# Cached keys turned by VectorE and attention biases added by VectorE in a streaming encoder

## What is computed

```python
q, k, v = split(x @ w_in); lf = log_sigmoid(x @ w_f + b_f)     # 16 heads of 64
c = cumsum(concat([cache_lf, lf]), axis=1)                      # prompt: no cache
s = q . k_all * 64 ** -0.5                                      # k_all = [cache_k, k]
s = s + cq[:, :, :, None] - ck[:, :, None, :]
s = where(kpos <= qpos, s, -inf)
o = softmax(s) . v_all;  y = o @ w_out
```

## Time and profile before

| | |
|---|---|
| runs, median (lowest to highest) | 1886.13 us (1880.18 to 1888.01) |
| profiled execution, first to last instruction | 1885.1 us |
| profiled execution, time around the span | none listed apart; the median of the runs is 1.0 us above the span |
| TensorE / VectorE / ScalarE / GpSimd busy | 98% / 52% / 38% / 12% |
| granted TensorE clock, mean | 0.997 |
| HBM read, written | 243.19 MB, 13.19 MB |

### The profile page before, as it was taken

One profiled execution on the slowest core, in us unless ns is written; L12 is line 12 of the kernel. 1 busy time (PEld: TensorE's weight loads), 2 busy tenths in 40 slices (PEclk: granted clock), 3 DMA queues, 4 the chain that ended last, 5 costly groups with the idle time before them and its releaser, 6 DMA issues.

```text
span 1885.1 us, 29064 instructions
## 1 busy us (share of the span) xinstructions
PE 1849.9 (98%) x12004; PEld 1642.4 (87%) x12004; DVE 983.0 (52%) x1569; ACT 722.0 (38%) x1144; POOL 225.9 (12%) x357
## 2 busy tenths in 40 slices
PE   8999999999999999999999999999999999999998
PEld 8777799998888887799998899998897777999986
DVE  4557653443567778743443664443465576543434
ACT  4246443333255454333332343333242463433321
POOL 3114070000011222230000100000031230000000
PEclk9999999999999999999999999999999999999999
DMA  7357254433353433444433434433364562444332
GB/s 246 128 203 229 81 160 123 129 129 123 117 164 105 125 116 104 118 139 125 124 134 123 146 101 125 132 124 125 110 206 150 200 221 90 137 132 124 128 129 79
DMA packets 179171, 259.38 MB, mean 138 GB/s; under 512 B 14717, under 2 KB 122349, under 8 KB 179040
## 3 DMA queue, kind: packets, MB, share of 16 engines
q1 hardware_dynamic: 161184, 197.18, 32.3%
q0 software_dynamic: 17856, 60.35, 9.9%
HBM read 243.19 MB, written 13.19 MB: 136 GB/s over the span
## 4 chain that ended last, share of the span: by engine, by line
PE 90%; DVE 4%; ACT 3%; issue 1%; DMA 1%; SPq 0%; DVEq 0%; ACTq 0%
PE ps L1605 14%; PE ps L1607 14%; PE ps L1606 14%; PE ps L1617 11%; PE ps L1615 11%; PE ps L1616 11%; PE ps L1833 1%; PE ps L1951 1%; PE ps L1938 1%; PE ps L1638 1%; PE ps L1888 1%; PE ps L1671 1%; DVE w_lo L785 1%; PE ps L1908 1%; PE ps L1673 1%
## 5 line engine op out<-in xcount | busy, mean ns | idle before, releaser
L785 DVE TENSOR_TENSOR w_lo<-w_raw,w_hi 128x1024 fp32r<-128x1024 f32 x370 | 452.1, 1228 | 709.1 <-ACT w_hi L439 707.9
L439 ACT ACTIVATE w_hi<-w_raw 128x1024 fp32r<-128x1024 f32 x370 | 389.3, 1059 | 803.5 <-DMA w_raw<-in_w_ffn_in_dram 363.1
L1605 PE MATMUL ps<-xT_hi,w_hi 128*128 128x384 f32 x1568 | 528.4, 337 | 2.5 <-issue 1.4
L1607 PE MATMUL ps<-xT_hi,w_lo 128*128 128x384 f32 x1568 | 527.0, 336 | 0.0
L1606 PE MATMUL ps<-xT_lo,w_hi 128*128 128x384 f32 x1568 | 526.9, 336 | 0.0
L1605 PEld LDWEIGHTS ps<-xT_hi,w_hi 128*128 128x128 f32 x1568 | 294.8, 188 | 5.2 <-issue 5.1
L1606 PEld LDWEIGHTS ps<-xT_lo,w_hi 128*128 128x128 f32 x1568 | 294.8, 188 | 0.1
L1607 PEld LDWEIGHTS ps<-xT_hi,w_lo 128*128 128x128 f32 x1568 | 294.8, 188 | 0.0
L1617 PE MATMUL ps<-w_hi,hT_lo 128*128 128x512 f32 x528 | 210.6, 399 | 0.0
L1616 PE MATMUL ps<-w_lo,hT_hi 128*128 128x512 f32 x528 | 208.1, 394 | 0.0
L1615 PE MATMUL ps<-w_hi,hT_hi 128*128 128x512 f32 x528 | 207.4, 393 | 0.0
(11 more groups left out here) (329 smaller groups left out, 2021.8 us busy)
## 6 DMA issues: line engine op xcount, KB each, us to landing
w_raw<-in_w_ffn_in_dram SPq DMA_DIRECT2D x352, 256.0 KB, 3.2
w_raw<-in_w_ffn_out_dram SPq DMA_DIRECT2D x176, 256.0 KB, 2.9
w_raw<-in_w_fox_in_dram SPq DMA_DIRECT2D x96, 256.0 KB, 2.9
k_c<-in_cache_fox_k_dram POOLq DMA_DIRECT2D x32, 512.0 KB, 5.3
v_c<-in_cache_fox_v_dram POOLq DMA_DIRECT2D x32, 512.0 KB, 4.0
w_raw<-in_w_hgrn_in_dram SPq DMA_DIRECT2D x64, 256.0 KB, 2.9
w_raw<-in_w_fox_out_dram SPq DMA_DIRECT2D x32, 256.0 KB, 2.9
out_dram<-kv_tok POOLq DMA_DIRECT2D x4, 1024.0 KB, 5.0
```

The costliest lines, as they stand in the source:

```text
L439: nc.scalar.activation(w_hi[:, slot, :], w_raw[:, slot, :], ACT.Copy).then_inc(hi_ready, 1)
L785: V.tensor_tensor(w_lo[:, slot, :], w_raw[:, slot, :], w_hi[:, slot, :].bitcast(F32), ALU.subtract).then_inc(lo_ready, 1)
L1605: mm(out, w_hi[:, slot, cols], x_hi[:, k, :], start=k == 0, stop=False, skip_group_check=True)
L1607: last = mm(out, w_lo[:, slot, cols], x_hi[:, k, :], start=False, stop=k == KD - 1, skip_group_check=True)
```

## The change

- The layer with `AHEAD = 3` is the second attention layer. Its cached keys are loaded by GpSimd during the feed-forward of layer 2 (8 loads of 1 MB, `cached_keys`), turned in blocks of 32x32 by VectorE (8 transposes of 128x256 in each of chunks 1 to 8, `turn_keys_ahead`), and stored turned by SP to a DRAM buffer `keys_t` (`store_turned`). In the attention loop SP loads them from there (`turned_keys`, 512 KB a set, three buffers), GpSimd adds the new keys' columns (`new_keys`), and TensorE's `s_keys` and the copies to `ktc` go.
- In both attention layers the sums are written to DRAM, read back broadcast over partitions (`load_prompt_bias`, 384 KB for two heads; `load_sample_bias`, 272 KB for a stream), masked by GpSimd, and added by VectorE in the instruction that also finds the extremum (`tensor_tensor_reduce`). Queries carry the opposite sign, so that the maximum becomes a minimum. The sum is written to SBUF, where ScalarE reads it.
- The bias and mask matmuls, and the constants and splits for them, go. TensorE's next scores wait for the extremum (`nmax`, `s_nmax`) and no longer for the exponential. In the second layer TensorE's folds move between the halves of `p_scores` and `p_out`, and the copies and low halves of the folds move later on ScalarE and VectorE.

The diff, cut to its core:

```diff
-CROWS = 64 + DT
-LAID = 17
+LAID = 4
+LOADED = 16 * 4
 KV = 3
+AHEAD = 3
+TWIN = 8
+TCOLS = 256
...
+            def turned_keys(i, first, end):
+                f = FOX[i]
+                for n in range(first, end):
+                    b, hf = n // 2, n % 2
+                    if n < KV:
+                        sync.wait_ge(*at(KEYS["stored"], 64 * DB))
+                        sync.wait_ge(unit_used, START[i]["mix"])
+                    else:
+                        sync.wait_ge(*at(f["s_scores"], n - KV + 1))
+                    sync.dma_start(k_t[:, n % KV, :, 0:PAST], keys_t[b, hf * WCOLS:(hf + 1) * WCOLS, :].rearrange(
+                        "(g p) k -> p g k", p=P)).then_inc(KEYS[f"in{n % KV}"][0], 16)
+            def store_turned(n):
+                b0, cols = 4 * (n // 4), slice(TCOLS * (n % 4), TCOLS * (n % 4) + TCOLS)
+                sync.wait_ge(*at(KEYS["turned"], n + 1))
+                for r in range(4):
+                    sync.dma_start(keys_t[b0 + r, cols, :].rearrange("(c d) k -> d c k", d=32),
+                                   k_turn[32 * r:32 * r + 32, :, :, :].rearrange("d c k a -> d c (k a)")).then_inc(KEYS["stored"][0], 16)
...
+                    if i + 1 == AHEAD and 3 <= c < CF:
+                        store_turned(c - 3)
...
+                    if i + 1 == AHEAD and 1 <= c <= DB:
+                        turn_keys_ahead(c - 1)
+            def turn_keys_ahead(n):
+                dve.wait_ge(*at(KEYS["loaded"], 16 * (n + 1)))
+                if n:
+                    dve.wait_ge(*at(KEYS["stored"], 64 * n))
+                for a in range(TWIN):
+                    ins = V.transpose(k_turn[:, :, :, a], k_nat[:, a, :])
+                ins.then_inc(KEYS["turned"][0], 1)
...
                     if 1 <= n <= HEADS:
                         dve.wait_ge(*at(f["s_scores"], n))
-                        V.tensor_reduce(nmx[:, (n - 1) % 2, 2:3], ps[:, SS_BANK, 0:PAST + DT], AX_X, ALU.max,
-                                        negate=True).then_inc(f["s_nmax"][0], 1)
+                        if n % 2:
+                            dve.wait_ge(*at(f["bias"], sample_bias(n // 2)))
+                        V.tensor_tensor_reduce(out=p_s[:, (n - 1) % 2, :], in0=ps[:, SS_BANK, 0:PAST + DT],
+                                               in1=bias_s[:, (n - 1) // 2 % 2, (n - 1) % 2, :], scale=1.0, scalar=LARGEST, op0=ALU.add,
+                                               op1=ALU.min, accum_out=nmx[:, (n - 1) % 2, 2:3]).then_inc(f["s_nmax"][0], 1)
...
                         dve.wait_ge(*at(f["scores"], n // 2 + 1))
-                        V.tensor_reduce(nmx[:, n % 2, 0:1], ps[:, bank, 0:P], AX_X, ALU.max, negate=True)
-                        V.tensor_reduce(nmx[:, n % 2, 1:2], ps[:, bank, P:T], AX_X, ALU.max,
-                                        negate=True).then_inc(f["nmax"][0], 1)
-                        if n:
+                        if n % 2 == 0:
+                            dve.wait_ge(*at(f["bias"], prompt_bias(n // 2)))
+                        for q, lo, hi in ((0, 0, P), (1, P, T)):
+                            ins = V.tensor_tensor_reduce(out=p_p[:, n % 2, lo:hi], in0=ps[:, bank, lo:hi],
+                                                         in1=bias_p[:, n // 2 % 2, n % 2, lo:hi], scale=1.0, scalar=LARGEST, op0=ALU.add,
+                                                         op1=ALU.min, accum_out=nmx[:, n % 2, q:q + 1])
+                        ins.then_inc(f["nmax"][0], 1)
+                        if n and i != AHEAD:
                             key_sides(n, KT_BANKS + 1)
...
+                def load_prompt_bias(k):
+                    pool.dma_start(bias_p[:, k % 2, :, :], sums_p[j, 2 * k:2 * k + 2, :].partition_broadcast(P)).then_inc(
+                        f["bias_in"][0], 16)
+                def load_sample_bias(b):
+                    pool.dma_start(bias_s[:, b % 2, :, :],
+                                   sums_s[j, :, b, :, :].rearrange("h f k -> h (f k)").unsqueeze(1).broadcast_to(
+                                       [HEADS // 2, DT, 2 * (PAST + DT)])).then_inc(f["bias_in"][0], 16)
+                def mask_prompt_bias(k):
+                    blocks = bias_p[:, k % 2, :, :].rearrange("p e (t c) -> p e t c", t=NTOK)[:, :, 0:NTOK:2, :]
+                    G.tensor_tensor(blocks, blocks, causal[:, :].unsqueeze(1).unsqueeze(1).broadcast_to([P, 2, 2, P]),
+                                    ALU.subtract).then_inc(f["bias"][0], 1)
+                def mask_sample_bias(b):
+                    new = bias_s[:, b % 2, :, PAST:]
+                    G.tensor_tensor(new, new, new_mask[:, :].unsqueeze(1).broadcast_to([P, 2, DT]), ALU.subtract).then_inc(
+                        f["bias"][0], 1)
+                def next_bias(m):
+                    if m:
+                        pool.wait_ge(*at(f["bias_in"], LOADED + 16 * (4 + m)))
+                        if m % 2:
+                            mask_prompt_bias(m // 2 + 2)
+                        else:
+                            mask_sample_bias(m // 2 + 1)
+                    if m < 2 * DB - 4 and m % 2 == 0:
+                        pool.wait_ge(*at(f["nmax"], m + 2))
+                        load_prompt_bias(m // 2 + 2)
+                    elif m < 2 * DB - 4:
+                        pool.wait_ge(*at(f["s_nmax"], m + 1))
+                        load_sample_bias(m // 2 + 2)
...
                 for n in range(KV, 2 * DB + KV):
-                    if n < 2 * DB:
+                    if n < 2 * DB and i == AHEAD:
+                        pool.wait_ge(*at(f["s_scores"], n - KV + 1))
+                        new_keys(n)
+                    elif n < 2 * DB:
                         pool.wait_ge(*at(f["ktr"], n - KV + 1))
                         load_k(n)
                     pool.wait_ge(*at(f["s_o"], n - KV + 1))
...
                     if n - KV + 2 < 2 * DB:
                         load_new(n - KV + 2)
+                    if n - KV <= 2 * DB - 4:
+                        next_bias(n - KV)
...
                 def p_scores(k):
-                    for e in range(2):
-                        h = 2 * k + e
-                        if k:
-                            pe.wait_ge(*at(f["exp"], h - 1))
-                        out = ps[:, S_BANK[e], 0:T]
-                        mm(out, sel_p[:, h:h + 1].broadcast_to([CROWS, P]), c_p[:, :], start=True, stop=False, skip_group_check=True)
-                        mm(out.rearrange("p (t c) -> p t c", t=NTOK)[:, 0:NTOK:2, :], ident_r[:, :],
-                           causal_r[:, :].rearrange("p (t c) -> p t c", t=NTOK)[:, 0:NTOK:2, :], start=False, stop=False,
-                           skip_group_check=True)
+                    if k:
+                        pe.wait_ge(*at(f["nmax"], 2 * k))
                     for lo, hi, n in ((0, P, P), (P, T, SEQ)):
+                        if lo and i == AHEAD and k:
+                            s_fold(2 * k - 2)
...
                 def s_pairs(n):
                     if n:
-                        pe.wait_ge(*at(f["s_exp"], n))
-                    pe.wait_ge(*at(f["kt_a"], n + 1))
-                    pe.wait_ge(*at(f["kt_d"], n + 1))
+                        pe.wait_ge(*at(f["s_nmax"], n))
+                    if i == AHEAD:
+                        pe.wait_ge(*at(KEYS[f"in{n % KV}"], 16 * (n // KV + 1)))
+                        pe.wait_ge(*at(KEYS["new"], n + 1))
+                    else:
+                        pe.wait_ge(*at(f["kt_a"], n + 1))
+                        pe.wait_ge(*at(f["kt_d"], n + 1))
...
-                    mm(ps[:, SS_BANK, 0:PAST + DT], sel_s[:, n % 2, :], c_s[:, n // 2, :], start=False, stop=True,
-                       skip_group_check=True).then_inc(f["s_scores"][0], 1)
+                    last.then_inc(f["s_scores"][0], 1)
```

More of the change, by code:

```diff
@@ L126, in trunk_program @@
         causal = sb("causal", [P, P], after("ident"))
-        ident_r = sb("ident_r", [P, P], after("causal"), F32R)
-        causal_r = sb("causal_r", [P, T], after("ident_r"), F32R)
-        fold = sb("fold", [P, 4, DT], after("causal_r"))
-        half = sb("half", [P, 2], after("fold"))
+        fold = sb("fold", [P, 4, DT], after("causal"))
+        new_mask = sb("new_mask", [P, DT], after("fold"))
+        half = sb("half", [P, 2], after("new_mask"))
         own = sb("own", [P, 2, HD], after("half"))
@@ L285, in trunk_program @@
             "z": 1, "zma": 2, "ze": 1, "zl": 1, "lf": 3, "cT": 5, "cT_ev": 5, "kT_done": KD, "kT_a": KD, "scores": KD,
[L286 removed]
+            "ones": 1, "c": 1 + DB, "laid": LAID, "bias_in": LOADED + 16 * 2 * DB, "bias": 2 * DB,
             **{k: HEADS for k in ("nmax", "exp", "rcp", "scaled", "pT", "pT_ev", "rcs")},
@@ L303, in trunk_program @@
         y_stored = sem("y_stored")
+        H = HGR[KINDS.index("hgrn")]
+        KEYS = {"loaded": (H["st0_in"][0], 16 * (HG // 2)), "stored": (x_in[0], 16),
```

(52 more changed lines are left out.)

183 lines of the change are left out of this document (96 added, 87 removed).

## The result

The change makes the kernel **slower**: 1949.04 us median (1948.4 to 1951.55, 4 runs) against 1885.43 of the kernel before on the same chip, ratio 1.0338, interval 1.032 to 1.0357. The forecast was 1871 in a range of 1860 to 1890. The profiled execution took 1948.72 us, its span 1946.7.

The account below looks back on a forecast made before the run. TensorE bounds the kernel before; after the change GpSimd's loop decides in both attention layers. Savings 6.6 + 8.9 = 15.5 us, other terms nothing: 1885.1 - 15.5 = 1869.6 traced, median 1870.6, say 1871; range 1860 to 1890.

Parts of the forecast that it names:

- The third feed-forward: VectorE's 64 key turns, 3.3 to 8.2 us a chunk, fit in 10.0 free of 16.7; SP's stores and added traffic cost nothing.
- without them each late microsecond is paid in full: Third feed-forward: without free VectorE time and the weights' lead of 21 us, each late microsecond costs its full length.
- Rival 5: Third feed-forward: turns or doubled traffic make weights late and eat the gain, 1886 us or more; chance 0.04.
- GpSimd's loop: Attention loops: one bias load in flight, landings 3.9 and 3.6 us, a pair 9.5; saves 6.6 and 8.9 us.
- it decides from about 4.5 us a landing: Attention loops: the slower outcome, Rival 4, decides once a bias load takes about 4.5 us to land.
- rivals 3: Attention loops: contention stretches both landings to 4.25 us, a pair is 10.5, 1.2 and 3.5 saved: 1881 us; chance 0.12.
- Rival 4: Attention loops: biases queue behind value loads, land in 5.3 us, a pair 12.6; 10.3 and 8.0 lost: 1904; chance 0.17.
- 3.6 us of first masks added: Before the attention loops: these masks lie beside the projection, where GpSimd idles 24.5 us, and cost nothing.
- The 34 us of matmuls: Attention loops: bias and mask matmuls, L1940 and second-layer key turns hold TensorE at most 20.0 + 14.1 = 34 us.
- by TensorE alone: Attention loops bound by TensorE: last scores end at 184.3 us (first layer) and 50.4 after the start (second), waits charged.
- A faster loop would meet it: Second attention layer: 17.8 MB of DMA at 329 GB/s take 54 us, no cost beside 59.
- Rival 2: Attention loops: sample bias moves on half the DMA engines, landing in 4.0 us for 3.6: 1875 us; chance 0.10.

Follow-up runs that it names:

- Experiment 1: Kernel after, with the stores of the turned keys issued by GpSimd behind its wait for the turns, SP neither waiting nor storing: 1911.15 us, ratio 1.0136.
- experiment 2: Experiment 1 with SP keeping its bare wait for the turns between weight loads: 1941.22 us, ratio 1.0299.
- kernel 10: The kernel of 8, with GpSimd issuing the next key load ahead of the four stores, nothing left out: 1880.08 us, ratio 0.9975.
- Experiments 3: Kernel after with the bias part alone; cached keys of the second layer turned by TensorE as in the kernel before: 1902.07 us, ratio 1.0093.
- 4: Kernel after, with GpSimd issuing the next bias load before it waits for and masks the previous, two in flight: 1930.52 us, ratio 1.0238.
- 5: Kernel after with the edits of Experiment 1 and 4 together: 1893.57 us, ratio 1.0044.
- 6: Experiment 1 without bias loads or later masks in the loops; later pairs and sets reuse the first biases, output wrong: 1875.41 us, ratio 0.9952.
- 8: Kernel before with only the keys part of the change, turned keys stored by GpSimd, biases still matmuls: 1886.65 us, ratio 1.0008.
- kernel 7: Experiment 1 with SP issuing the loop's bias loads, one of each kind in flight, GpSimd only masking: 1890.49 us, ratio 1.0035.

## Why the prediction was wrong

**The step that failed** is "The third feed-forward", which ends "I cost it at nothing". It is 39 of the 62 us. Its sizes held: the turns are 0.51 us each from start to start inside the bounds of 0.41 and 1.03, and VectorE had the time. What failed is the sentence "SP's stores wait for the turns amid weight loads, but those run five units, 21 us, ahead". It took the weights' lead as cover for a single delay and did not ask what the released turn itself waits for. Weights behind SP's wait stand ahead of the next turn in VectorE's list: wait and release form a ring, and a ring has a period, not a lead. Experiment 1 shows it by opening the ring, and experiment 2 by closing it again with the bare wait. The price after it, "without them each late microsecond is paid in full", was too low as well: 24.0 us of waiting brought 15.4 more at the lower clock, a term that the prediction did not have. Rival 5 named this stage and late weights, at 0.04 and "1886 or more". The weights were late, but because SP held them back, not by the time of the turns or by traffic: kernel 10 has all of both and takes 266.8 us.

**The second failed term** is the landings in "GpSimd's loop". The mechanism, one bias load in flight and GpSimd's loop as the last to arrive, was right, and the landings, 4.8 us on the mean of both kinds, lie beyond the threshold it gave: "it decides from about 4.5 us a landing". The sizes were off: 5.2 and 4.3 us for 3.9 and 3.6. The rows of a lone load stood for loads that follow a key and a value load; no run times a bias load alone, so how much of the miss that is stays open. The pair is 11.0 us, not 9.5, in between rivals 3 and 4. Rival 4 forecast losses of 10.3 and 8.0 us; they are 8.8 and 13.1. In the second layer the landings are longer (5.9 and 5.2 us), and its first pair takes 13.2 us for 9.3, at the lower clock. Experiments 3 and 4 bear out the mechanism, 5 that it is independent of the ring.

**A small term put at nothing:** "3.6 us of first masks added" was to lie beside the projection. But GpSimd's masks stand behind the same wait for ScalarE's `kT` as the zeroing and the copy of new values that the loop's start needs. The earlier trace rows have the zeroing at 122.28; in the kernel after, the masks begin at 123.42 and it follows at 126.98. In the second layer the copy goes out 1.3 us behind the first sample maximum, where it went out 5.5 ahead of it, and TensorE waits 2.2 us for it. No run takes the masks away from there.

**TensorE's own bound was too low.** The 34 us of matmuls did go, but the waits charged at 0.2 us a pair and 0.35 a step were too small: 8.7 us a pair for 8.5 in the first layer, 8.2 for 7.4 in the second. With no bias loads in the loop (6) the layers gain 5.2 and 9.1 where "by TensorE alone" had 8.7 and 17.5 with the turns outside the loop. The keys alone give 4.6 (8). So 14.3 of the 34 us were to be had. That the removed matmuls had covered latencies of ScalarE and VectorE fits the waits for ScalarE in 6, but they are a part of the idle time only.

**The DMA sum was noticed and priced at nothing.** "A faster loop would meet it" is what kernel 7 did, at a DMA share of 0.97: its second layer's pairs take 10.0 us, more than the 9.5 before.

**Right:** masks of 1.27 and 0.25 us for 1.6 and 0.2; the new operation at 0.44, with 0.08 more to read the minimum out; GpSimd waiting for DMA before each mask, and VectorE for GpSimd at the head of a pair; the stages without an edit unchanged. Rival 2 drew on the Trainium skill, "DMA: Bandwidth & Descriptors", section "Why a DMA increments its semaphore by 16 and not by 1". It stays open. With one load in flight the 272 KB load with 8 outermost landed in 4.3 us and the 384 KB one in 5.2. But with two in flight (4) the smaller one was the slower, 7.5 to 6.5, and so were the first two of each, issued in a row ahead of the first loop of the kernel after: 8.8 to 5.3. There it also stands behind the larger ones, so no run separates its shape from the loads around it.

## What to carry to other kernels

Before putting a wait into a queue that loads ahead, follow what stands behind it until you either reach an engine that never comes back to the releaser, or close a ring; of a ring, sum the period and compare it with the bound of the stage, for a lead hides it only for the first rounds. Issue a store from the queue that already waits for its producer, and within that queue put the load that the next round needs ahead of the stores. A matmul that is removed from a loop of short dependent steps gives back only what it did not cover: measure the loop with the new transport taken out before paying for that transport. And where a stall is followed by a lower clock, price it at more than its length.

## What was not expected of the hardware

TensorE's clock fell after short stalls, so that a stall costs more than its length. Windows of the kernel after: the first microsecond after a wait of 4.3 us, the next three, the rest of the chunk, then two stretches of the second attention loop.

```profile
1193.90:1195.10 1.20, 1.14 (x6) 1.14 (x7) 0.29 (x2) 1.16 (x2) 0.00 (x0) 0.90 0.00 0
1195.10:1198.20 3.10, 3.10 (x12) 3.10 (x11) 3.10 (x7) 1.58 (x2) 0.00 (x0) 0.50 0.01 3
1198.20:1208.00 9.80, 9.80 (x58) 9.80 (x58) 3.74 (x6) 0.00 (x0) 0.88 (x1) 1.00 0.71 176
...
1537.00:1540.00 3.00, 0.98 (x7) 0.73 (x7) 1.77 (x10) 2.25 (x9) 2.68 (x5) 0.93 0.73 243
1540.00:1550.00 10.00, 8.47 (x80) 5.59 (x80) 2.72 (x13) 3.42 (x13) 3.06 (x8) 0.51 0.91 317
```

Single matmuls in the second and the third of these windows:

```profile
1196.27 0.52 PE L1748 MATMUL ps<-xT_hi,w_hi 128*128 128x384 f32 x1
1196.59 0.52 PE L1749 MATMUL ps<-xT_lo,w_hi 128*128 128x384 f32 x1
...
1200.32 0.34 PE L1748 MATMUL ps<-xT_hi,w_hi 128*128 128x384 f32 x1
1200.50 0.34 PE L1749 MATMUL ps<-xT_lo,w_hi 128*128 128x384 f32 x1
```

At 0.50 (1.2 GHz) a matmul starts 0.32 us after the one before it, at 1.00 (2.4 GHz) 0.17. After each of the six stalls at a chunk's head (3.2 to 4.4 us) they start 0.32 apart for 3.4 to 6.2 us, though TensorE is busy without a gap: from 1.5 us lost here to some 3, and 15.4 in the whole stage, 2.6 a stall. The Trainium skill, "TensorE: Matmul & The Clock Gate", section "Part 1: The HAM clock gate", says that the gate knows half and full rate only; the windows of 0.50 and 1.00 agree. In the second attention loop TensorE was busy for 0.98 of the 3 us from 1537 to 1540, and from 1540 to 1550 it ran at 0.51 though it was busy 85% of that time. This differs between kernels whose code is nearly the same there. In the kernel after, 1, 2 and 4 TensorE waits 1.4 to 2.3 us for the first copy of new values and then runs ten us at 0.51 to 0.56: the first pair takes 12.7 to 13.5 us. In 5, 6 and 7 it doesn't wait there, the clock is 0.87 to 0.92, and the pair takes 9.1 to 9.3. So the second attention layer holds some 4 us of this in the kernel after, 1, 2 and 4; why these kernels and not the others is open.

Two more: kernel 6's loop, with no bias load in it, runs the DMA at 257 GB/s and 0.75 in the second layer, so the room for any added traffic there was a quarter; and kernel 7 reached 0.97 at 299 GB/s, below the 329 GB/s that the earlier trace rows gave for a full share.
